# A modulation slab moved behind the third of the key, value and query slabs, in the seam ahead of the latent attention

## The chip, the cores and the metric

The kernel runs on one core of one Trainium2 chip. The metric is the device time of one execution in microseconds. The program is compiled once; the weights lie in the chip's memory and are streamed in while the kernel computes.

## What is computed

A hybrid block (gated linear attention beside block attention, then a convolutional feed-forward network) is followed by a two-layer block that is modulated by a condition. The change lies in its second layer, between the feed-forward network of the first layer and the window attention of the second, on 256 latent tokens of 1024 features:

```python
mod_lat = (sc @ ada_w[i] + ada_b[i])[:, None, :]
sh1, sc1, g1, sh2, sc2, g2 = jnp.split(mod_lat, 6, axis=-1)
a_lat = modulate(rmsnorm_2(h_lat, norm1_g[i]), sh1, sc1)
...
qc, kc, vc = split_qkv(h_ctx, w_qkv)
q, k, v = split_qkv(h_lat, w_qkv)
q = apply_rope(q, cos, sin) * scale
k = apply_rope(k, cos, sin)
```

`ada_w` has 6144 output columns for each layer. Only the part with `sh1` and `sc1` is needed ahead of the attention; the rest is computed wherever the order has room for it.

## The kernel before

**Slabs.** Every weight matrix is stored as slabs of 128 partitions x 2048 fp32 (1 MB): all 1024 rows of 256 output columns. SyncE streams them in an order fixed by `RUN_ORDER` into a ring of three slots of `raw`. Most slabs are split into two parts for TensorE: ScalarE writes the upper part `whi` (L822, the function `hi`), VectorE and GpSimd each half of the lower part `wlo` (L1300 `lo`, L780), and each product is then three matmuls (`mm3`, L1913 to L1915). A modulation slab is not split: `ada_group` multiplies it from `raw` with the condition `cnd`, 8 fp32 matmuls that appear as 16 records (L2059), and adds its row to bank 3 of `ps`.

**The ring.** A slot is loaded again when the slab in it is no longer needed in `raw`: for a split slab when both halves of `wlo` are there, for a modulation slab when TensorE has used it. SyncE issues the loads strictly in stream order, so a load that waits holds up all behind it.

```python
if g.c >= RING and (g + -RING).whole:
    sp.wait_ge(slab_done, (g + -RING).number() + 1)
elif g.c >= RING:
    sp.wait_ge(lo_done, (g + -RING).split() + 1)
    sp.wait_ge(lo2_done, (g + -RING).split() + 1)
```

**The seam.** Call the six slabs of keys, values and queries Q0 to Q5 and the five streamed modulation slabs A0 to A4 (in the code `("qkv", i)` and `("ada_c", i)`; four more modulation slabs of the same group lie aside, so A0 to A4 are numbers 4 to 8 in `ada_group`). They are loaded in the order Q0 A0 Q1 A1 Q2 A2 Q3 A3 Q4 A4 Q5, then the output slabs `wo` 0 to 3. With three slots, A3 goes where Q2 was, Q4 where A2 was, A4 where Q3 was, and Q5 where A3 was. TensorE uses them in another order, written out by hand: A0, A1, Q0 and Q1 mixed, A2, A3, the rotation of the keys (`turn`, L2350), Q2, A4, Q3 with the rotation of the first queries between its two halves, Q4, Q5. `EARLIER` says at which place of the used slabs each modulation slab is counted, so that the waits on `slab_done` count rightly; it has to agree with the calls.

**ScalarE's order in the seam.** For each i from 0 to 5 it first splits a slab ahead (i = 0: Q3, i = 1: Q4, i = 2: Q5), then waits until TensorE has used Qi, and copies its result out of `ps`: i = 0 to `mv` (`kv_sb` = 2, L1198), i = 1 to `state` (`kv_sb` = 3, L1200), i = 2 and later to `sra` (`q_sb`, L1202). TensorE waits for `kv_sb` = 2 ahead of the rotation of the keys, for `kv_sb` = 3 ahead of the modulation slabs behind Q2, and for `q_sb` = 1 ahead of the rotation of the first queries in the middle of Q3.

Of the kernel before, what the change touches and what calls it, by code (L numbers as in the profile page):

```python
# [102 lines left out]
def ada_bank(i):  # L103
# [18 lines left out]

EARLIER = [(("ada_a", 0), ("pw2_ctx", 3))] + [(("ada_a", k + 1), ("pw1_lat", k)) for k in range(7)] + [
    (("ada_b", 0), ("pw2_lat", 3)), (("ada_b", 1), ("k_ctx", 0)), (("ada_b", 2), ("v_ctx", 0)),
    (("ada_c", 0), ("qkv", 0)), (("ada_c", 1), ("qkv", 0)), (("ada_c", 2), ("qkv", 2)), (("ada_c", 3), ("qkv", 2)),
    (("ada_c", 4), ("qkv", 3))]


# [138 lines left out]
def build(nc, io):  # L267
# [10 lines left out]
    with ctx:  # L278
# [489 lines left out]
        def _(pool):  # L768
# [37 lines left out]
            for use, _, _, count in RUN_ORDER[1:]:  # L806
                run(c, use, 0, count)
                c += count
# [1101 lines left out]
        def _(pe):  # L1910
# [12 lines left out]
            def features(g, bank, x, kts=KT, tiles=2, split=None, lo_sem=xlo_done, between=None):  # L1923


                if split is not None and lo_sem is xlo_done:
                    upper_halves(g, bank, x, split, tiles)
                    lower_halves(g, bank, x, split, tiles)
                    return
                w = weights(g, kts)  # L1930
                for m in range(tiles):
                    if m and between:
                        between()
                    for k in range(kts):
                        if split is not None and m == 0 and k % 2 == 0:
                            pe.wait_ge(lo_sem, KT // 2 * split + k // 2 + 1)
                        ins = mm3(ps[:, bank + m // 2, (m % 2) * T:(m % 2) * T + T],
                                  [a[:, k, m * P:m * P + P] for a in w], [a[:, k, :] for a in x],
                                  start=(k == 0 and m % 2 == 0), stop=(k == kts - 1))
                ins.then_inc(slab_done, 1)  # L1940
# [32 lines left out]
            def lower_tokens(g, bank, x):  # L1973

                w = whi[:, g.slot, :].rearrange("p (k n) -> p k n", k=KT)
                for s in range(2):
                    for k in range(KT):
                        ins = pe.matmul(ps[:, bank, s * T:s * T + T], x[1][:, k, s * P:s * P + P], w[:, k, :],
                                        start=False, stop=(k == KT - 1), skip_group_check=True)
                ins.then_inc(slab_done, 1)  # L1980
# [68 lines left out]
            def ada(g, bank, k=0, n=1):  # L2049

                pe.wait_ge(landed[g.slot], g.landings())
                ada_rows(raw[:, g.slot, :], bank, k, n).then_inc(slab_done, 1)

            def ada_rows(slab, bank, k, n):

                w = slab.rearrange("p (k n) -> p k n", k=KT)
                for t in range(KT):
                    r, c = QUAD * (t % 4), cnd_at + QUAD * t - 2 * k
                    ins = pe.matmul(ps[r:r + QUAD, bank, 0:SLABC], cnd[:, c:c + QUAD], w[:, t, :], start=(t < 4 and k == 0),  # L2059
                                    stop=(t >= 4 and k == n - 1), skip_group_check=True)  # L2060
                return ins
# [10 lines left out]
            def ada_group(use, k0, k1):  # L2072

                for k in range(k0, k1):
                    n, first = ASIDE.get(use, 0), sum(ASIDE[u] for u in GROUPS[:GROUPS.index(use)] if u in ASIDE)
                    if k < n:
                        pe.wait_ge(aside_landed, 16 * (first + n))
                        ada_rows(aside[ASIDE_AT[use][k]], GROUP_BANKS[use][0], k, GROUP_SLABS[use][1]).then_inc(aside_done, 1)
                    else:
                        ada(Slab(PLACE[use, k - n]), GROUP_BANKS[use][0], k, GROUP_SLABS[use][1])  # L2080
# [261 lines left out]
            upper_tokens(Slab(PLACE["qkv", 1]), 1, H)  # L2342
            lower_halves(Slab(PLACE["qkv", 0]), 0, H, 7)
            lower_tokens(Slab(PLACE["qkv", 1]), 1, H)
            ada_group("ada_c", 6, 8)

            def turn(raw_, bank, done):

# [24 lines left out]
            def turn_q(j):  # L2373

                pe.wait_ge(q_sb, j + 1)
                if j == 3:
                    pe.wait_ge(q_ready, 3)
                turn(q_raw[:, 2 * j:2 * j + 2, :], (5, 6, 7, 7)[j], qrot_done)
# [14 lines left out]

            features(Slab(PLACE["qkv", 2]), 0, H)
            pe.wait_ge(kv_sb, 3)
            ada_group("ada_c", 8, 9)
            features(Slab(PLACE["qkv", 3]), 1, H, between=lambda: turn_q(0))
            features(Slab(PLACE["qkv", 4]), 2, H, between=beside_third)
            pe.wait_ge(k_ready, 1)
# [268 lines left out]
```

## Time and profile before

| | |
|---|---|
| median of 3 runs | 1404.03 us (1402.92 to 1407.85) |
| profiled execution: own time | 1407.16 us |
| profiled execution: span | 1405.4 us |
| TensorE busy | 1374.8 us, 98% |
| VectorE, ScalarE, GpSimd busy | 977.6, 821.5 and 569.0 us |
| share of the chain that ended last | TensorE 86%, VectorE 5%, DMA 4% |
| mean granted TensorE clock | 0.996 |

The span runs from the first to the last instruction of the profiled execution; the own time holds what lies around it too. The chain that ended last is followed back from the last instruction, at each step to what released it.

### The profile page before, as it was taken

What the parts mean: (1) busy time and instruction counts of PE and PEld (TensorE: products, weight loads), DVE (VectorE), ACT (ScalarE), POOL (GpSimd) and SP (SyncE); (2) the same over time, 40 slices, a digit from 0 to 9 for tenths busy, and PEclk for the clock granted to TensorE, in tenths of its full rate; (3) what the DMA queues carried; (4) which work ended last, traced back from release to release, by engine and by line L of the source; (5) the groups of instructions that cost most, each with busy time, mean ns of one, the idle gap of its engine ahead of it and who ended that gap; (6) DMA issues with size and microseconds to landing.
All of it is one profiled execution on the core that took longest, in us unless ns stands there. A gap on an engine that the chain in (4) does not pass through costs nothing.

```text
span 1405.4 us, 27626 instructions
## 1 busy us (share of the span) xinstructions
PE 1374.8 (98%) x10866; PEld 1286.1 (92%) x10866; DVE 977.6 (70%) x1302; ACT 821.5 (58%) x1179; POOL 569.0 (40%) x190
## 2 busy tenths in 40 slices
PE   7999999999999999999999999999999999999997
PEld 4778889999999999899999999999998868899997
DVE  3312674847899988669899979766666695666665
ACT  3632565645788836566888565544445486544443
POOL 2443436455232223452222223666653303466661
PEclk9999999999999999999999999999999999999999
DMA  8675774455344434674444456655555604354550
GB/s 323 253 287 205 260 283 182 154 194 196 131 180 179 172 155 183 248 294 153 157 164 159 173 202 247 233 217 209 209 180 184 263 34 142 140 196 183 179 179 31
DMA packets 39430, 271.01 MB, mean 193 GB/s; under 512 B 4596, under 2 KB 5876, under 8 KB 6958
## 3 DMA queue, kind: packets, MB, share of 16 engines
q1 hardware_dynamic: 39342, 269.76, 51.7%
q8 instruction: 64, 1.05, 0.3%
q14 instruction: 24, 0.20, 0.0%
HBM read 268.68 MB, written 1.06 MB: 192 GB/s over the span
## 4 chain that ended last, share of the span: by engine, by line
PE 86%; DVE 5%; DMA 4%; ACT 3%; POOL 1%; issue 1%; SPq 0%; DVEq 0%; ACTq 0%
PE ps L1913 22%; PE ps L1914 22%; PE ps L1915 22%; PE ps L636 9%; DMA raw<-w_dram 4%; PE ps L2059 3%; PE ps L1950 1%; ACT whi L822 1%; POOL wlo L780 1%; PE ps L2427 1%; PE ps L2413 1%; PE ps L1960 1%; PE ps L2022 1%; ACT mqk L906 1%; DVE wlo L1300 1%
## 5 line engine op out<-in xcount | busy, mean ns | idle before, releaser
L780 POOL TENSOR_TENSOR wlo<-raw,whi 128x1024 fp32r<-128x1024 f32 (+1 forms) x181 | 566.7, 3134 | 812.1 <-ACT whi L822 812.0
L822 ACT ACTIVATE whi<-raw 128x2048 fp32r<-128x2048 f32 x181 | 345.6, 1911 | 399.5 <-PE ps L1915 224.7
L1300 DVE TENSOR_TENSOR wlo<-raw,whi 128x1024 fp32r<-128x1024 f32 (+1 forms) x181 | 277.8, 1535 | 305.5 <-ACT whi L822 304.5
L1913 PE MATMUL ps<-h_hi,whi 128*128 128x256 f32 x1232 | 354.8, 288 | 2.8 <-ACT gates L979 2.0
L1914 PE MATMUL ps<-h_lo,whi 128*128 128x256 f32 x1232 | 349.1, 283 | 0.0
L1915 PE MATMUL ps<-h_hi,wlo 128*128 128x256 f32 x1232 | 349.1, 283 | 0.0
L1913 PE MATMUL ps<-g_hi,whi 128*128 128x256 f32 x1040 | 298.5, 287 | 2.4 <-POOL wlo L780 1.5
L1914 PE MATMUL ps<-g_lo,whi 128*128 128x256 f32 x1040 | 294.2, 283 | 0.0
L1915 PE MATMUL ps<-g_hi,wlo 128*128 128x256 f32 x1040 | 294.2, 283 | 0.0
L1913 PEld LDWEIGHTS ps<-h_hi,whi 128*128 128x128 f32 x1232 | 236.8, 192 | 10.8 <-issue 6.6
L1914 PEld LDWEIGHTS ps<-h_lo,whi 128*128 128x128 f32 x1232 | 236.9, 192 | 0.4
L1915 PEld LDWEIGHTS ps<-h_hi,wlo 128*128 128x128 f32 x1232 | 236.8, 192 | 0.0
L1913 PEld LDWEIGHTS ps<-g_hi,whi 128*128 128x128 f32 x1040 | 199.4, 192 | 6.8 <-issue 5.3
L1914 PEld LDWEIGHTS ps<-g_lo,whi 128*128 128x128 f32 x1040 | 199.4, 192 | 0.4
L1915 PEld LDWEIGHTS ps<-g_hi,wlo 128*128 128x128 f32 x1040 | 199.4, 192 | 0.0
L636 PE MATMUL ps<-cvb,raw 128*128 128x256 f32 x704 | 155.3, 379 | 0.0
L636 PEld LDWEIGHTS ps<-cvb,raw 128*128 128x128 f32 x704 | 132.5, 190 | 17.3
L1914 PE MATMUL ps<-m_lo,whi 128*128 128x256 f32 x384 | 108.7, 283 | 0.0
L1913 PE MATMUL ps<-m_hi,whi 128*128 128x256 f32 x384 | 108.7, 283 | 0.0
L1915 PE MATMUL ps<-m_hi,wlo 128*128 128x256 f32 x384 | 108.7, 283 | 0.0
L553 DVE SCALAR_TENSOR_TENSOR cvb<-ps,cols,cvb 128x255 f32<-128x255 f32 (+1 forms) x176 | 76.5, 476 | 11.3 <-ACT cvb L475 6.7
L553 DVE SCALAR_TENSOR_TENSOR cva<-ps,cols,cva 128x255 f32<-128x255 f32 (+1 forms) x176 | 76.6, 476 | 9.4 <-ACT cva L475 4.2
(295 smaller groups left out, 1879.4 us busy)
## 6 DMA issues: line engine op xcount, KB each, us to landing
raw<-w_dram SPq DMA_DIRECT2D x243, 1024.0 KB, 4.9
sra<-w_dram SPq DMA_DIRECT2D x2, 1024.0 KB, 6.4
mqk<-w_dram SPq DMA_DIRECT2D x2, 1024.0 KB, 6.4
brev<-w_dram SPq DMA_DIRECT2D x2, 1024.0 KB, 6.8
gates<-w_dram SPq DMA_DIRECT2D x2, 1024.0 KB, 8.4
xlat<-xT_dram SPq DMA_DIRECT2D x2, 512.0 KB, 4.6
brev<-w_first_keys_dram SPq DMA_DIRECT2D x1, 1024.0 KB, 8.9
brev<-bias_rows SPq DMA_DIRECT2D x1, 1024.0 KB, 9.4
```

What stands on the lines that cost most here:

```text
L553: ins = dve.scalar_tensor_tensor(out, ps[:, 2 * par + half, m * T + src:m * T + src + n], w, out, ALU.mult, ALU.add)
L636: ins = pe.matmul(ps[:, 4 + m // 2, (m % 2) * T:(m % 2) * T + T], wf[:, k, m * P:m * P + P], cvb[:, par, k, :], start=(first and k == 0 an ...
L780: pool.tensor_tensor(wlo[:, g.slot, part], raw[:, g.slot, part], whi[:, g.slot, part].bitcast(F32), ALU.subtract).then_inc(lo2_done, 1)
L822: act.activation(whi[:, g.slot, :], raw[:, g.slot, :], ACT.Copy).then_inc(hi_done, 1)
L906: act.activation(ctx_sq[:, t * T:t * T + T], acc[:, t, :], ACT.Silu, scale=col("ln_g", t), bias=col("ln_b", t)).then_inc(act_done, 1)
L1300: dve.tensor_tensor(wlo[:, g.slot, part], raw[:, g.slot, part], whi[:, g.slot, part].bitcast(F32), ALU.subtract)\
L1913: pe.matmul(out, w[0], x[0], start=start, stop=False, skip_group_check=True)
L1914: pe.matmul(out, w[0], x[1], start=False, stop=False, skip_group_check=True)
L1915: return pe.matmul(out, w[1], x[0], start=False, stop=stop, skip_group_check=True)
L1950: pe.matmul(ps[:, bank, m * T:m * T + T], w[i][:, k, m * P:m * P + P], x[0][:, k, :], start=(k == 0 and m == 0 and i == 0), stop=False, sk ...
L1960: ins = pe.matmul(ps[:, bank, m * T:m * T + T], w[:, k, m * P:m * P + P], x[1][:, k, :], start=False, stop=(k == KT - 1), skip_group_check ...
L2059: ins = pe.matmul(ps[r:r + QUAD, bank, 0:SLABC], cnd[:, c:c + QUAD], w[:, t, :], start=(t < 4 and k == 0), stop=(t >= 4 and k == n - 1), s ...
```

## The change

In `ada_group`'s calls A3 (number 7) moves from ahead of Q2, where it stood with A2, to behind Q2, where it stands ahead of A4. The count in `EARLIER` moves with it. Nothing is added or taken away, and the order of the loads stays.

```diff
-    (("ada_c", 0), ("qkv", 0)), (("ada_c", 1), ("qkv", 0)), (("ada_c", 2), ("qkv", 2)), (("ada_c", 3), ("qkv", 2)),
+    (("ada_c", 0), ("qkv", 0)), (("ada_c", 1), ("qkv", 0)), (("ada_c", 2), ("qkv", 2)), (("ada_c", 3), ("qkv", 3)),
     (("ada_c", 4), ("qkv", 3))]
...
             lower_tokens(Slab(PLACE["qkv", 1]), 1, H)
-            ada_group("ada_c", 6, 8)
+            ada_group("ada_c", 6, 7)
...
             features(Slab(PLACE["qkv", 2]), 0, H)
             pe.wait_ge(kv_sb, 3)
-            ada_group("ada_c", 8, 9)
+            ada_group("ada_c", 7, 9)
             features(Slab(PLACE["qkv", 3]), 1, H, between=lambda: turn_q(0))
```

On TensorE, behind Q1 and ahead of Q2, this is the order (the first two rows are A2, the two taken away are A3, L2350 is the rotation of the keys):

```order
 L2059 MATMUL ps<-raw,cnd 32x256 [waits slab_landed2]
 L2059 MATMUL ps<-raw,cnd 32x256 x7
-L2059 MATMUL ps<-raw,cnd 32x256 [waits slab_landed1]
-L2059 MATMUL ps<-raw,cnd 32x256 x7
 L2350 MATMUL ps<-mv,gates 128x256 [waits kv_copied,tables_landed]
 L2350 MATMUL ps<-mv,gates 128x256
```

The wait for A3's landing and its eight matmuls no longer stand between A2 and the rotation. Behind Q2, whose last rows are the first two here, the order on TensorE is this (`kv_copied` is `kv_sb`; `slab_landed1` is A3's slot, `slab_landed0` A4's; the last row is Q3's first):

```order
 L1914 MATMUL ps<-h_lo,whi 128x256
 L1915 MATMUL ps<-h_hi,wlo 128x256
-L2059 MATMUL ps<-raw,cnd 32x256 [waits slab_landed0,kv_copied]
+L2059 MATMUL ps<-raw,cnd 32x256 [waits slab_landed1,kv_copied]
+L2059 MATMUL ps<-raw,cnd 32x256 x7
+L2059 MATMUL ps<-raw,cnd 32x256 [waits slab_landed0]
 L2059 MATMUL ps<-raw,cnd 32x256 x7
 L1913 MATMUL ps<-h_hi,whi 128x256 [waits slab_lo_done_by_gpsimd,slab_lo_done_by_vector]
```

A3's matmuls now stand here, and the wait for the copy of the values (`kv_copied`) has moved from A4 to A3. The instructions of the other engines stay in their order; SyncE's wait ahead of Q5's load is still the one for A3's use, and its count is one higher.

## Rows read from the trace of the kernel before

**Rows 1.** The head of the page: span, TensorE's busy time.
```profile
span 1405.4 us, 27626 instructions
PE 1374.8 (98%) x10866; PEld 1286.1 (92%) x10866; DVE 977.6 (70%) x1302; ACT 821.5 (58%) x1179; POOL 569.0 (40%) x190
```

**Rows 2.** The chain of waits through the seam: start us, us, what.
```profile
1074.30 10.49 DMA raw<-w_dram
...
1084.82 1.92 ACT whi L822
...
1086.81 3.40 POOL wlo L780
...
1090.65 8.24 DMA raw<-w_dram
...
1098.91 1.91 ACT whi L822
1100.82 0.49 ACT sra L1202
```

**Rows 3.** Timeline of TensorE in the seam: start us, us, [idle before <-releaser].
```profile
1086.30 1.07 PE L2059 MATMUL ps<-raw,cnd 128*32 128x256 f32 x16
1089.08 1.07 PE L2059 MATMUL ps<-raw,cnd 128*32 128x256 f32 x16 [1.72 <-DMA raw<-w_dram]
1090.08 1.13 PE L2350 MATMUL ps<-mv,gates 128*128 128x256 f32 x4
...
1096.88 1.07 PE L2059 MATMUL ps<-raw,cnd 128*32 128x256 f32 x16
1097.88 0.39 PE L1913 MATMUL ps<-h_hi,whi 128*128 128x256 f32 x1
...
1101.36 1.13 PE L2350 MATMUL ps<-sra,gates 128*128 128x256 f32 x4 [0.35 <-ACT sra L1202]
```

**Rows 4.** Timeline of ScalarE in the seam.
```profile
1086.63 0.58 ACT L1198 ACTIVATE mv<-ps 128x512 f32<-128x512 f32 x1
1092.19 1.92 ACT L822 ACTIVATE whi<-raw 128x2048 fp32r<-128x2048 f32 x1 [4.98 <-DMA raw<-w_dram]
1094.01 0.58 ACT L1200 ACTIVATE state<-ps 128x512 f32<-128x512 f32 x1
```

**Rows 5.** Timeline of SyncE: the load of Q4 is issued.
```profile
1087.43 0.33 SPq L676 DMA_DIRECT2D raw<-w_dram  x1
```

**Rows 6.** DMA issues: KB each, median us to landing; Q4; A4; Q2; A4 and Q5.
```profile
raw<-w_dram SPq DMA_DIRECT2D x1, 1024.0 KB, 4.7
...
raw<-w_dram SPq DMA_DIRECT2D x1, 1024.0 KB, 4.8
...
raw<-w_dram SPq DMA_DIRECT2D x1, 1024.0 KB, 5.3
...
raw<-w_dram SPq DMA_DIRECT2D x2, 1024.0 KB, 6.5
```

**Rows 7.** Timeline of TensorE at two other places where it stood idle.
```profile
87.74 0.56 PE L1913 MATMUL ps<-h_hi,whi 128*128 128x256 f32 x1 [2.02 <-ACT gates L979]
...
91.09 0.35 PE L1913 MATMUL ps<-h_hi,whi 128*128 128x256 f32 x1
91.27 0.28 PE L1914 MATMUL ps<-h_lo,whi 128*128 128x256 f32 x1
91.39 0.28 PE L1915 MATMUL ps<-h_hi,wlo 128*128 128x256 f32 x1
...
1202.74 0.36 PE L1950 MATMUL ps<-h_hi,whi 128*128 128x256 f32 x1 [1.57 <-ACT h_hi L848]
```

**Rows 8.** Stretches: us, PE busy (x), PEclk, DMA share, GB/s.
```profile
88.00:89.00 1.00, 1.00 (x6) 0.50 0.95 401
1088.00:1089.00 1.00, 0.00 (x0) 1.00 0.92 221
```

**Rows 9.** TensorE's longest waits behind the seam, 1101.5 to 1190 us.
```profile
PE ps L2362 <- ACT tiny L1190: 0.6, 2, 0.4
```

## Prediction

> **What bounds the kernel now.** The page's head comes first [rows 1]: TensorE is busy for 1374.8 us of a span of 1405.4, so a change that removes no TensorE work is worth at most the idle time that it takes away, and costs whatever idle time it makes. The timeline of TensorE shows the idle time that the change can reach [rows 3]. A2 begins at 1086.30 and is through at 1087.36 or 1087.37; then the engine stands for 1.72 us until A3 has landed, at 1089.08. The second gap is 0.35 us ahead of the rotation of the first queries at 1101.36. Together that is 2.07 us, all that there is to gain between 1086 and 1102 us. Behind it, up to 1190 us, no wait for a transfer is among TensorE's waits; the longest group is 0.6 us for ScalarE [rows 9].
>
> The chain of waits over the same stretch says something that the timeline does not [rows 2]. It does not run through TensorE's matmuls at all: it goes from the load of Q3 (10.49 us, to 1084.8) to its split on ScalarE and GpSimd (to 1090.21), to the load of Q5 (issued 1090.65, landed 1098.89), to ScalarE's split of Q5 (from 1098.91), and to its copy of the first queries (from 1100.82), which TensorE has to have at 1101.36. The 1.72 us gap is therefore not on the path that sets the end. Had A3 been there in time, TensorE would have reached the middle of Q3 sooner and waited for the same copy. What has to move earlier, if anything is to be gained, is the landing of Q5.
>
> **The change, part by part.** No instruction is added or removed. Four things move.
>
> *The gap for A3 goes.* TensorE goes from A2 straight to the rotation of the keys. The rotation needs ScalarE's copy to `mv`, which begins at 1086.63 and takes 0.58 [rows 4], so is there at 1087.21; the rotation starts at 1087.36 instead of 1090.08. From the rotation's start to A4's start were 1096.88 - 1090.08 = 6.80 us of unbroken work [rows 3], so Q2 ends at 1087.36 + 6.80 = 1094.16. The gain here is 2.72 us, 1.72 of waiting and 1.00 of A3's work put off.
>
> *The wait for the copy of the values.* Behind Q2 stands the wait for `kv_sb` = 3. ScalarE makes that copy behind its split of Q4, which waits for Q4's landing: the split begins at 1092.19, the copy at 1094.01, and it ends at 1094.59 [rows 4]. Neither moves, since Q4's load is released by A2's use and is issued at 1087.43 as before [rows 5]. TensorE can start A3 0.04 later, at 1094.63: a new wait of 0.47 us. Before, this wait was covered by A3 and its gap. A3 and A4 follow, 1.00 us each (1089.08 to 1090.08 in [rows 3]); A4's load goes out when GpSimd's split of Q3 ends at 1090.21 [rows 2], ahead of Q5's, and lands 4.8 us later [rows 6], near 1095.1, before it is wanted at 1095.63. Q3 starts at 1096.63, still 1.25 us earlier than the 1097.88 of [rows 3].
>
> *The load of Q5.* Its slot is A3's. SyncE may issue it only when TensorE has used A3. Before, this had happened at 1090.1 and the load went out at 1090.65, right behind A4's. Now A3 ends at 1094.63 + 1.07 = 1095.70, and with the 0.06 between A2's end (1087.37) and the issue at 1087.43 [rows 3, 5] the load goes out at 1095.76, 5.11 us later. Part of that comes back, because Q5 had stood in the queue behind A4: the pair has a median of 6.5 us, A4 itself 4.8, so Q5 took 8.2 [rows 6], the 8.24 of [rows 2]. A load with nothing ahead of it took 4.7 (Q4), 4.8 (A4), and 5.3 with two behind it (Q2) [rows 6]. When Q5 goes out, A4 has landed. I take 4.8: Q5 lands at 1100.56, not at 1098.89. The ends are 4.7 and 8.2, 8.2 if the output slab that is issued about 2 us behind it takes an equal share; the nearest row is the 4.8 of A4, which had Q5 0.4 us behind it, so such a share is unlikely.
>
> *From there to TensorE.* From Q5's landing to the rotation of the first queries were 1101.36 - 1098.89 = 2.47 us, the split, the copy and the hand-overs [rows 2, 3]. They are in ScalarE's order and don't shrink. The rotation starts at 1100.56 + 2.47 = 1103.03 instead of 1101.36: 1.67 us later. With 4.7 it is 1.57, with 5.3 2.17, with 8.2 5.1.
>
> TensorE meanwhile has nothing else to do. The first half of Q3 took from 1097.88 to 1101.01 (1101.36 less 0.35), 3.13 us; it now ends at 1096.63 + 3.13 = 1099.76, and the engine stands still for 3.27 us. That leads to the last term.
>
> *The granted clock.* Where TensorE stood for 2.02 us ahead of 87.74, the granted clock read 0.50 in the stretch behind it, which is the level of 1.2 GHz [rows 7, 8]. Where it stood for 1.72 us (up to 1089.08) and 1.57 us (up to 1202.74) the matmuls behind ran on at 2.4 GHz; the clock read 1.00 at 1088 to 1089 [rows 3, 7, 8]. So the gap of 3.27 us is longer than one that cost the clock, while both that are there near this place were shorter. At 87.74 the 15 matmuls up to 91.09 took 3.35 us, where at 0.12 each (91.27 to 91.39) they take 1.80: 1.55 us lost [rows 7]. I take this in full. Below, it can be nothing; above, about 1.7, half of that 3.35 us stretch.
>
> The Trainium skill says the same of the cause (TensorE: Matmul & The Clock Gate, section What's actually happening): the clock is halved when the array has been idle, and comes back after activity. By that rule the drop is to be expected here, and the trace agrees at 87.74 with its 0.50.
>
> Against this change speaks a rule of the Trainium skill (DMA: Bandwidth & Descriptors, section Rules for kernel authors): issue the transfer early, wait for it late. The change makes one wait later (A3) and one issue later (Q5). The same page's section on the anatomy of one DMA gives about 2.0 us fixed plus the bytes at 436 GB/s, which makes 4.4 us for 1 MB, an estimate; the sum would be 0.4 us smaller by it. The trace has 4.7 to 4.8, and that is used.
>
> **What is late next.** Q5's lower part on GpSimd ends 1.67 us later, but ahead of Q5 TensorE still has the second half of Q3 and both halves of Q4 to do, three times some 3.1 us. The output slab whose slot is Q5's is loaded later by the same amount and used only in the output product behind the attention. Everything else behind 1101.36 follows TensorE and moves with it. I see no wait there that ends at a time of its own, so nothing is given back [rows 9].
>
> **Sum.** 1.67 + 1.55 = +3.2 us. The profiled execution would go from 1407.16 to 1410.4. It stood 3.1 us above the median of the runs shown, so the same sum on the median gives 1404.03 + 3.2 = **1407.2 us**, 0.23% more. About 0.5% (7 us) is what a measurement of this kernel can tell from no change; the three runs alone span 4.9 us.
>
> **Rivals.**
> *The clock holds.* The gap is as worked out, but the granted clock stays at 1.00 behind it. For it: two gaps of 1.6 to 1.7 us went by unpunished [rows 3, 7]. Against it: a gap of 2.02 us did not. Time: 1404.03 + 1.67 = 1405.7.
> *Faster.* The two gaps go, and the first queries' copy is in time. This is one mechanism: Q5's landing decides. The copy would have to be ready at 1099.76, when the first half of Q3 ends, so Q5 landed at 1097.3, which from an issue at 1095.76 leaves 1.5 us for 1 MB; to break even with before it would need to land at 1098.89, 3.1 us after its issue. No row is under 4.7. It could only be if the chain of waits misleads, for example if the copy waits for TensorE and not for the split ahead of it. Then 2.07 us are saved less the 0.47 of the new wait: 1402.4.
> *Q5's load is shared.* The output slab's load goes out about 2 us behind Q5 and both move together, or A4 is late and Q5 behind it: Q5 takes 8.2 us as it did before [rows 6]. Then TensorE stands for 6.7 us and the clock drops: 1404.03 + 5.1 + 1.6 = 1410.7. Against it: loads with a later one close behind took 4.8 and 5.3.
> *No effect.* SyncE, ScalarE and VectorE keep their order, and something else could carry the same end time. The chain leaves 0.02 to 0.04 us at each hand-over, so there is no room for another cause. It falls in with the clock rival in time.
>
> **How the numbers follow.** Late Q5 with the clock drop 0.60; late Q5 without it 0.22; faster 0.08; shared load 0.08; something else 0.02. The time is that of the first. The range takes the first two and the spread of the runs around a median, and reaches toward the others: 1402.5 to 1410.5. All cases named lie within 0.5% of before (1397.0 to 1411.0), the shared load just so; I give 0.04 to slower by over 0.5%, 0.02 to faster by over 0.5%, and 0.94 to the rest.
>
> **What the changed profile would show.** Right: no idle time ahead of the rotation of the keys, which starts 2.7 us earlier, counted from the start of A2; a wait of some 0.5 us for the copy to `state` ahead of A3; SyncE's load of Q5 about 8.3 us behind that of Q4; ahead of L2350 on `sra` a wait of about 3.3 us for ScalarE's copy; and a granted clock of 0.50 for some 3 us behind it. Wrong: Q5 landed as early as before, the wait at L2350 under 2 us, the clock at 1.00 behind it, or TensorE idle elsewhere in the attention.

## The result, and the profile after

Measured together, the changed kernel took a median of 1408.32 us (1405.81 to 1413.39, 20 runs) and the kernel before 1405.82 us (1402.92 to 1411.81, 20 runs). The ratio is 1.0021, with a 95% interval of 1.0011 to 1.0030: about 3.0 us slower (0.0021 x 1405.82); the medians themselves lie 2.5 us apart. The forecast was +3.2 us, from 1404.03 to 1407.2. Its starting point was the median of three runs, which lies 1.8 us under that of all 20; the difference is what the forecast can be judged by.

The profiled execution of the changed kernel has a span of 1404.2 us, 1.2 us less than that of before [rows 1], although the kernel is slower. So whole spans are not the thing to compare. A2's start lies at 1083.42 us where it lay at 1086.30, and nothing ahead of A2 was edited. The executions differ there in the clock: over the first 100 us the granted clock was 1.00 here and 0.97 in the one of before, and 0.03 of 100 us is about the 2.9 us that A2 starts sooner. Whether that is chance comes up again under what stays open. What the edit does is read from A2's start onward.

First the timeline of TensorE in the seam of the changed kernel (start us, us, idle before and what ended it), the same places as [rows 3]:

```profile
1083.66 0.83 PE L2059 MATMUL ps<-raw,cnd 128*32 128x256 f32 x12
1084.42 1.13 PE L2350 MATMUL ps<-mv,gates 128*128 128x256 f32 x4
...
1091.85 1.94 PE L2059 MATMUL ps<-raw,cnd 128*32 128x256 f32 x32 [0.56 <-ACT state L1200]
1093.71 0.39 PE L1913 MATMUL ps<-h_hi,whi 128*128 128x256 f32 x1
...
1100.16 1.13 PE L2350 MATMUL ps<-sra,gates 128*128 128x256 f32 x4 [3.31 <-ACT sra L1202]
```

The first line begins inside A2 (a window cuts it). The rotation of the keys follows it with no gap: the 1.72 us for A3 are gone. A3 and A4 stand together behind Q2 (32 records) after 0.56 us for the copy of the values. The rotation of the first queries waits 3.31 us for ScalarE. From A2's start to this rotation are 1100.16 - 1083.42 = 16.74 us; before, 1101.36 - 1086.30 = 15.06 [rows 3]. That is +1.68.

The chain of waits over the same stretch answers to [rows 2]:

```profile
1084.55 4.83 DMA raw<-w_dram
1089.40 1.91 ACT whi L822
1091.31 0.49 ACT state L1200
...
1091.85 1.11 PE ps L2059 x16
1092.98 4.71 DMA raw<-w_dram
...
1097.72 1.91 ACT whi L822
1099.63 0.49 ACT sra L1202
```

The path has a new first half. It was Q3's load, its split, Q5's load [rows 2]. Now it is Q4's load, its split on ScalarE, the copy of the values behind it, A3 on TensorE (the 16 records), and only then Q5's load. Q5's load itself is short, 4.71 us instead of 8.24, with nothing ahead of it in the queue. It is issued 8.43 us behind Q4's, where it had been 3.22 (1090.65 less 1087.43 in [rows 2, 5]).

The clock did not drop behind the gap in this execution (us, busy, granted clock, DMA share, GB/s), so it shows the first term of the sum alone:

```profile
1097.00:1098.00 1.00, 0.00 (x0) 1.00 0.96 393
...
1101.00:1102.00 1.00, 1.00 (x10) 1.00 1.00 426
```

### The profile page after: what moved, and what is told of

Same layout as the page of the kernel before. It is cut to its first block, busy times and chain, and to the rows that moved or that the text cites. A ratio compares the mean times of both kernels' runs of the same rounds, so it can differ in the third digit from the quotient of the medians.

```text
span 1404.2 us, 27626 instructions
## 1 busy us (share of the span) xinstructions
PE 1371.7 (98%) x10866; PEld 1284.6 (91%) x10866; DVE 980.8 (70%) x1302; ACT 821.5 (59%) x1179; POOL 568.9 (41%) x190
## 4 chain that ended last, share of the span: by engine, by line
PE 86%; DVE 5%; ACT 3%; DMA 3%; issue 1%; POOL 1%; SPq 0%; DVEq 0%; ACTq 0%
PE ps L1913 22%; PE ps L1914 22%; PE ps L1915 22%; PE ps L636 9%; DMA raw<-w_dram 3%; PE ps L2059 2%; PE ps L1950 2%; ACT whi L822 1%; PE ps L2427 1%; PE ps L1960 1%; PE ps L2413 1%; POOL wlo L780 1%; DVE wlo L1300 1%; ACT mqk L906 1%; PE ps L2362 1%
## 5 line engine op out<-in xcount | busy, mean ns | idle before, releaser
L1300 DVE TENSOR_TENSOR wlo<-raw,whi 128x1024 fp32r<-128x1024 f32 (+1 forms) x181 | 281.0, 1553 | 303.5 <-ACT whi L822 302.5
```

What stands on the lines that cost most here:

```text
L1300: dve.tensor_tensor(wlo[:, g.slot, part], raw[:, g.slot, part], whi[:, g.slot, part].bitcast(F32), ALU.subtract)\
```

## The experiments

Two theories. Mine: Q5's landing sets when the first queries are rotated, the change delays it by making its slot free later, and the gap that this opens costs the granted clock in part of the executions. The rival: A3's place on TensorE or the wait for the copy of the values costs, and Q5's load only looks guilty. Twelve more runs were made in three batches (E1 to E4, E5 to E8, E9 to E12), each batch beside a set of runs of the kernel before of its own, so the ratios of a batch share whatever chance lies in that set. Some of the twelve repeat a kernel. Beside the ratios the table gives two distances in each profile: from A2's start to the rotation of the first queries, and from A2's start to the end of the span. They are free of what happens ahead of the seam. The end of a span is read to 0.1 us.

| kernel | ratio to before [95%] | A2 to rotation | A2 to end |
|---|---|---|---|
| before | 1 | 15.06 | 319.10 |
| changed | 1.0021 [1.0011, 1.0030] | 16.74 | 320.78 |
| E1 Q5's load released by Q2 | 1.0044 [1.0029, 1.0060] | 17.45 | 322.97 |
| E2 copy ahead of split | 1.0013 [1.0003, 1.0024] | 13.26 | 318.65 |
| E3 gap filled | 1.0030 [1.0018, 1.0042] | 16.68 | 320.70 |
| E4 changed, again | 1.0038 [1.0023, 1.0054] | 16.75 | 322.28 |
| E5 before, again | 1.0003 [0.9991, 1.0015] | 15.00 | 319.11 |
| E6 A3 ahead of the wait | 1.0029 [1.0013, 1.0045] | 16.13 | 322.89 |
| E7 all ahead | 0.9973 [0.9956, 0.9990] | 13.06 | 317.07 |
| E8 before, copy ahead of split | 0.9989 [0.9979, 0.9999] | 14.68 | 318.72 |
| E9 gap filled, again | 1.0023 [1.0009, 1.0038] | 16.76 | 320.80 |
| E10 changed, a third time | 1.0021 [1.0010, 1.0032] | 16.71 | 322.28 |
| E11 copy ahead, again | 0.9998 [0.9985, 1.0011] | 13.37 | 318.71 |
| E12 copy and rotation ahead | 0.9996 [0.9985, 1.0007] | 13.42 | 317.45 |

### E1: only the release of Q5's load, nothing moved on TensorE

```diff
+                if isinstance(g.j, int) and g.c == PLACE["qkv", 5]:
+                    sp.wait_ge(slab_done, done("qkv", 2))
-                if g.c >= RING and (g + -RING).whole:
+                elif g.c >= RING and (g + -RING).whole:
```

> The kernel before, with one wait changed: SyncE issues Q5's load only when TensorE has used Q2, not A3. TensorE's order is that of before, so A3 is not moved. My theory (the landing of Q5 sets the end): Q2 ends at 1096.9 on the scale of the trace of before, Q5 lands 4.8 us later, ScalarE's copy is there 2.5 us after that, so the rotation of the first queries starts near 1104.2 instead of 1101.4, with a wait of some 3.1 us ahead of it: +2.8 us against before, up to +4.3 with a drop of the granted clock. The rival (A3's place on TensorE costs, by itself or through the wait for the values' copy): within 0.5 us of before.

Here TensorE's order is that of before. The chain of waits:

```profile
1097.92 4.78 DMA raw<-w_dram
1102.73 1.91 ACT whi L824
1104.64 0.49 ACT sra L1204
```

The rotation comes 17.45 us behind A2's start, 2.39 later than before, with 3.22 us of waiting ahead of it (expected 2.8 later; A3's gap was 1.21 us instead of 1.72 in this execution, which takes 0.5 off). The late release alone makes the delay; the rival's "within 0.5 us" fails, in the profile and in the ratio. The clock dropped behind this gap too, 1.4 us after TensorE had started again.

### E2 and E11: the copy of the first queries ahead of ScalarE's split of Q5

```diff
+            COPY_FIRST = (2,)
...
-                if i < RING:
+                if i < RING and i not in COPY_FIRST:
                     c = hi_to(c, "qkv", i + RING)
                 act.wait_ge(slab_done, done("qkv", i))
...
+                if i in COPY_FIRST:
+                    c = hi_to(c, "qkv", i + RING)
```

The edit is made on the changed kernel. For i = 2 the split no longer stands first; it comes right behind the copy.

> The changed kernel, with ScalarE's copy of the first queries ahead of its split of Q5. My theory (TensorE waits for Q5's landing only because the copy stands behind the split): the 3.3 us wait ahead of the rotation of the first queries goes, and the rotation starts about 1.6 us earlier than in the kernel before; the split of Q5 now holds up VectorE's rotation of the first queries, which may give back up to 1.5 us ahead of the first scores. Against before: -1.6 to 0 us; against the changed kernel: -1.7 to -4.5. The rival (the copy waits for TensorE's Q2, or a landing nearer to TensorE is late): the wait stays at 3.3 us, and the time is that of the changed kernel.

Q5's load is as late as in the changed kernel, but TensorE no longer waits for it. The rotation starts 13.26 us behind A2's start, 1.80 ahead of before and 3.48 ahead of the changed kernel. So it was ScalarE's order, the split and then the copy, that tied the queries' rotation to a load that it doesn't use. VectorE's order gives most of it back, as feared; this is the timeline of TensorE in the second run of this kernel, ahead of the first scores:

```profile
1105.47 0.50 PE L2365 MATMUL ps<-m_hi,g_hi 64*128 64x512 f32 x2 [1.31 <-DVE g_lo L1782]
```

From A2 to the end it is 0.45 us ahead of before, yet the ratio was 1.0013 and its interval left out 1. That called for a second run:

> The changed kernel with the copy of the first queries ahead of the split of Q5, once more, since its profile (0.45 us ahead of before from A2 to the end) and its times (ratio 1.0013) disagreed. If the profile is right: ratio 0.9990 to 1.0005. If there is a cost that this one profile doesn't show, a drop of the clock behind the new wait of 1.3 us for instance: 1.0013 again with a mean clock under that of before.

It gave 0.9998, and 0.39 us in the profile. The two profiles agree, the two ratios only within their intervals. The mean granted clock over the runs was lower than that of the kernel before both times, by 0.0013 in E2 and by 0.0005 in E11 (standard error of each 0.0004 to 0.0005). So the first ratio was in part the clock. Whether the clock falls behind the new wait of 1.3 us in some executions, as the expectation asks, stays open: it did in neither profile (1.00 behind both waits).

### E12: VectorE's rotation ahead of its share of the split too

```diff
-                if i < RING:
+                if i < RING - 1:
                     c = lo_to(c, "qkv", i + RING)
...
                 if i in (3, 4):
                     rope_q(i - 3)
+                if i == 3:
+                    c = lo_to(c, "qkv", 5)
```

> The same, with VectorE's rotation of the first queries ahead of its share of Q5's split too; A3 stays behind the wait. My theory (the 1.3 us wait ahead of the first scores in the kernel with the copy first comes from VectorE's order): that wait goes, the first scores come 21.3 us behind A2's start (22.6 with the copy first alone, 23.1 before), and the end is 1.8 us nearer than in the kernel before, ratio 0.9987. The rival (it is ScalarE's order that makes the scores late): the wait of 1.3 us stays.

The wait of 1.3 us is gone, and the end lies 317.45 us behind A2, 1.65 ahead of before (expected 1.8). The ratio, 0.9996 [0.9985, 1.0007], just takes in the expected 0.9987 but can't tell it from no change. The mean granted clock was that of the kernel before (0.9971 against 0.9969).

### E6: A3 ahead of the wait for the copy of the values

```diff
+            ada_group("ada_c", 7, 8)
             pe.wait_ge(kv_sb, 3)
-            ada_group("ada_c", 7, 9)
+            ada_group("ada_c", 8, 9)
```

> The changed kernel, with A3 ahead of TensorE's wait for the copy of the values and A4 behind it. My theory (Q5's load follows A3's use): A3 and with it Q5's load, its landing and the rotation of the first queries all come 0.5 us earlier, so the rotation starts 16.2 us behind A2's start where the changed kernel has 16.7, and the wait ahead of it stays at some 3.3 us. Against before +1.1 us, and the clock may still drop. The rival (the wait for the values' copy is what costs, not the load): with that wait gone from A3's place the rotation starts at 15.1 us or earlier.

The rotation starts 16.13 us behind A2 instead of 16.74, and the wait ahead of it is still 3.34 us. The load follows A3's use: 0.61 us less ahead of A3 is 0.61 us less to the rotation. The wait for the copy costs only as much as it puts off A3.

### E3, E4, E9 and E10: what the gap costs beside its length

E3 fills the gap of the changed kernel with matmuls that nothing uses:

```diff
+            def filled_turn():
+                w = whi[:, Slab(PLACE["qkv", 3]).slot, :].rearrange("p (k n) -> p k n", k=KT)
+                for n in range(26):
+                    pe.matmul(ps[:, 7, 0:T], w[:, n % KT, 0:P], h_hi[:, n % KT, :], start=(n == 0), stop=(n == 25),
+                              skip_group_check=True)
+                turn_q(0)
...
-            features(Slab(PLACE["qkv", 3]), 1, H, between=lambda: turn_q(0))
+            features(Slab(PLACE["qkv", 3]), 1, H, between=filled_turn)
```

> The changed kernel, with 26 extra matmuls of 0.12 us each (3.1 us) into an unused bank between the first half of Q3 and the rotation of the first queries: they fill the idle time and leave the chain through Q5's load alone. If a drop of the granted clock behind the gap makes part of the loss, the time is 1.7 us above before (ratio 1.0012) and about 1.3 us under the changed kernel. If the gap alone is the loss, it is the time of the changed kernel within 0.5 us. In both cases the rotation of the first queries stays where it is, 16.7 us behind the start of A2.

> The changed kernel once more, beside the others on the same chip. Theory with a clock drop in part of the executions: ratio to before 1.0012 to 1.0030, mean granted clock 0.001 lower than before or so. Theory of the gap alone: ratio 1.0012, 1.7 us, and the same mean clock. In the profile the wait ahead of the rotation of the first queries is 3.3 us in both; by the first the clock behind it reads 0.50 in some profiles.

In E4's profile the clock fell near the end of the gap. The stretches behind it show it (the same columns as above), and so does the rotation, 2.08 us for its four records where it was 1.13:

```profile
1097.00:1098.00 1.00, 0.00 (x0) 1.00 0.94 385
1098.00:1099.00 1.00, 0.00 (x0) 0.94 1.10 459
1099.00:1100.00 1.00, 0.83 (x2) 0.50 0.95 401
...
1101.00:1102.00 1.00, 1.00 (x6) 0.50 0.07 25
1102.00:1103.00 1.00, 1.00 (x9) 0.85 0.00 0
```

```profile
1099.17 2.08 PE L2350 MATMUL ps<-sra,gates 128*128 128x256 f32 x4 [3.35 <-ACT sra L1202]
```

With its parts of the stretches at 0.94 and 0.85 the clock stayed at 0.50 for 3.4 us. A2 to rotation is the same as without the drop (16.75 against 16.74). A2 to end is 322.28 instead of 320.78: 1.50 us for the drop, in all +3.18 against before. In E3 the work between reads as one row, and the wait that is left is 0.21 us:

```profile
1097.19 3.28 PE L2383 MATMUL ps<-h_hi,whi 128*128 128x256 f32 x26
1100.68 0.70 PE L2350 MATMUL ps<-sra,gates 128*128 128x256 f32 x2 [0.21 <-ACT sra L1202]
```

It ends 320.70 us behind A2. In these profiles the filling saves nothing of the first term and all of the second. The two were repeated together:

> The changed kernel with 26 extra matmuls in the gap, once more, beside the changed kernel on the same chip (the next run). With the clock as a part of the loss: mean granted clock 0.001 above the changed kernel's and its time at least 1 us lower. With the gap alone: both equal within 0.5 us and 0.0003 of the clock.

> The changed kernel a third time: ratio to before between 1.0012 (no execution drops the clock) and 1.0024 (all do); the rotation of the first queries 16.7 us behind A2's start.

E9's profile ends 320.80 us behind A2, E10's 322.28 with another drop, which here began 1.5 us after the rotation had started. The times are less clear. Filled and changed kernel stood at 1.0030 and 1.0038 in the first pair, at 1.0023 and 1.0021 in the second, and neither pair tells them apart; the gain of 1 us that was expected of E9 is not shown. The mean granted clock over all runs was 0.9956 for the changed kernel (43 runs, standard error 0.0002), 0.9967 for the filled one (23 runs, 0.0003) and 0.9969 for the kernel before (97 runs, 0.0001). That is the sign expected, though within the second pair the difference is only 0.0005; the size, 0.0011 x 1404 = 1.5 us, fits a drop in most executions.

The clocks on record also say how much of a ratio is clock, from any place in the kernel. Within the three sets of the kernel before, a run whose mean clock is lower by 0.001 is about 1.4 us longer (a straight line through the 97 runs). Set against before at equal clock by that line, the mean times are +2.6 us (E4) and +1.7 (E10) for the changed kernel, +3.0 (E3) and +2.2 (E9) for the filled one, +1.4 for E6 and -2.5 for E7, each good to about 0.5 us; as they stand they are +5.4, +2.9, +3.8, +2.8, +3.6 and -3.3. So what the changed kernel loses beyond the 1.68 of its first profile is mostly clock. For the filled kernel, whose profiles end 1.6 and 1.7 us behind before, some 0.9 us is left over.

### E5, E8 and E7: the kernel before, and the version that gains

> The kernel before, entered as a kernel under test. It shows how far two sets of runs of one program lie apart here. Both theories: ratio 1.0000 within its interval, the rotation of the first queries 15.1 us behind the start of A2, the end 319.1 us behind it.

The kernel before against itself: ratio 1.0003, and 15.00 and 319.11 us in the profile where the first had 15.06 and 319.10. In it A3's gap was 1.18 us and the later wait for ScalarE 0.81, against 1.72 and 0.35 [rows 3]. One gap grew by what the other lost, and the rotation did not move. A gap on the path that shrinks by 0.54 us would have brought the rotation forward by as much; it moved by 0.06. So the gap for A3 was not on the path.

> The kernel before, with only ScalarE's copy of the first queries put ahead of its split of Q5; A3 stays ahead of Q2. My theory: this takes the seam's path off Q5's landing, but the gap for A3 still stands, so only the 0.35 us ahead of the rotation of the first queries goes: the end 318.8 us behind A2's start against 319.1, ratio 0.9997. The rival (the order of the copy by itself moves the time): more than 1 us either way.

It came 0.38 us nearer to the end (expected 0.3), with a ratio of 0.9989 [0.9979, 0.9999], which takes in the expected 0.9997; at equal clock its mean time is 0.6 us under before, good to 0.5 us. The untouched gap for A3 is 1.83 us here.

E7 joins E6 and E12, on the changed kernel (their diffs, nothing else).

> The changed kernel with A3 ahead of the wait, ScalarE's copy of the first queries ahead of its split of Q5, and VectorE's rotation of the first queries ahead of its share of that split. My theory: no wait on TensorE is left in the seam; the rotation of the first queries starts 12.7 us behind A2's start (15.06 in the kernel before) and the first scores 20.8 us behind it (23.09 before): -2.3 us against before. The rival (the split of Q5, now later, is missed elsewhere): a wait ahead of Q5 or of the first scores gives back 1 us or more.

Its rotation starts 13.06 us behind A2 and its end lies 317.07 behind it, 2.03 us ahead of before (expected 2.3), with no wait left in the seam. The ratio is 0.9973 [0.9956, 0.9990]: it beats both kernels. With the path off Q5's landing, moving A3 behind Q2 does what removing its gap should do, and the 2.03 us are nearly the 2.07 that the two gaps of before held. The kernel before with both new orders, ScalarE's and VectorE's, was not run; that the order on VectorE would give it nothing is argued from E8, where A3's gap is the only wait left in the seam.

## Why the prediction was right

*The gap for A3 goes, and isn't worth anything.* Right. TensorE reached the rotation of the keys 2.78 us sooner (3.78 and 1.00 behind A2), for which 2.72 was forecast, and nothing came of it. E5 shows the gap off the path, E2 and E7 what it takes to make it count.

*The wait for the copy of the values.* Forecast 0.47 us, measured 0.56, and 0.53 and 0.50 in E4 and E10.

*The load of Q5.* Forecast 4.8 us in flight, measured 4.71; E1 makes it the cause. The output slab issued 1.91 us behind it took no share. The 4.4 us that the prediction works out from the Trainium skill (DMA: Bandwidth & Descriptors, section Anatomy of one DMA) come from a fit for transfers issued from GpSimd, while SyncE issues these; the measured 4.71 decides. The sum to the rotation was +1.67 by the forecast and +1.68 in the profile; the wait ahead of it 3.27 forecast and 3.31 measured.

*The granted clock.* Forecast 1.55 us, taken in full. The drop cost 1.5 us in E1, E4 and E10 (in E1 305.52 us from the rotation to the end, 304.04 where no drop came). So the price, read at another place, was right. That it is due each time was not. Of the five profiles with a gap over 3.2 us in the seam it came in four, E1, E4, E6 and E10, and not in the first profile of the changed kernel. And in E6 the clock stayed down twice as long, from 1097.7 to 1104.5 us, and cost 2.7 us (306.76 less 304.04):

```profile
1099.00:1100.00 1.00, 1.00 (x3) 0.50 1.00 426
...
1103.00:1104.00 1.00, 1.00 (x7) 0.50 0.49 156
1104.00:1105.00 1.00, 1.00 (x8) 0.74 1.04 442
```

So this term should have been an average over 0, 1.5 and 2.7, each with its chance, and no single value. The five profiles average 1.4 us, near the 1.55 taken, so the sum came out near although the term is no constant. The prediction read the one gap of 2.02 us that cost the clock as the sign that a longer one would. Length alone doesn't decide: outside the seam a gap of 1.94 us (E1, at 198 us) had a drop behind it and one of 2.36 us (E12, at 198 us) had none. The Trainium skill (TensorE: Matmul & The Clock Gate, section What's actually happening) says that the chip's watch on TensorE's activity runs freely and is not set back when a kernel starts. That agrees with one program showing the drop in two profiles (0.50) and not in a third (1.00).

*Nothing is given back.* Right: behind the rotation all kernels need 304.0 to 304.1 us to the end, before and changed, where neither a drop nor E2's later wait comes between.

*The rivals.* The clock holding was right for one profile, not for most. "Faster" failed as priced: the load would have had to land within 3.1 us and took 4.71. The shared load (8.2 us) did not occur.

What stays open: the ratios of the changed kernel (1.0021, 1.0038 and 1.0021) have a mean of about 3.8 us, above the 3.2 of a profile with one drop. At equal clock the excess is within the error in E10 and twice that in E4, so drops elsewhere and longer ones as in E6 can fill most of it. The filled kernel keeps some 0.9 us more than its profiles give, and for that I have no cause. The distances from A2 don't see what lies ahead of it, and there the profiles differ: A2 starts at 1086.3 to 1087.7 us in the four profiles with A3 ahead of Q2, at 1082.4 to 1085.5 in the ten with A3 behind it, a difference that has opened within the first 210 us. The mean clock over all runs, 0.9969 for the kernel before and 0.9956 for the changed one, gives no sign that this holds outside the profiled executions, but no run shows where it comes from. The control (1.0003 with a half width of 0.0012) says that about 1.7 us of any single ratio can be the measurement.

## What to carry to other kernels

Before a gap is closed, follow the chain of waits past it. A gap that another load covers is worth nothing, and here moving its work took the slot of the load that mattered. When an in-order engine makes a result available, look at what stands ahead of it in its queue: a copy of 0.6 us behind a split that waits for a transfer inherits the transfer's lateness. And when a ring slot is freed by the consumer, every later place of that consumer is a later issue, to be charged with the load's full time in flight.

## What the runs showed of the hardware

A gap of 3.3 us on TensorE costs the clock in some executions of one program and not in others, for one stretch of 3.4 us (1.5 us lost) or for 6.8 us (2.7 us lost). The fall can come before the gap ends (E4, E6) or 1.4 to 1.5 us after TensorE has started again (E1, E10), so the first matmuls behind a gap can still be fast. Behind gaps of 1.2 to 1.8 us in this seam (before, E1, E2, E5, E8, E11) the clock stayed at 1.00.

Q5's load of 1 MB took 4.71 to 4.78 us with the queue empty in all nine profiles whose chain holds it so, and Q4's 4.74 to 4.98, so where Q5's load went out fixed its landing to 0.1 us, while whole spans of the changed kernel lay at 1404 to 1405 us in profiles and its times at 1404.9 to 1415.9 us.
